# Query, key and value projections by seven products in pairs, instead of twelve tiles of eight

## The reference, cut to what matters

```python
h = concatenate([meta, x])                  # 16 + 512 = 528 tokens, 1024 channels
xn = rmsnorm(h, norm1_g)
q, k, v, xr, gr, g_merge = split(xn @ w_in) # q: 8 heads of 128, k and v: 2 heads each
q = axial_rope(rmsnorm(q, q_norm_g))        # norm over the 128 channels of a head
k = axial_rope(rmsnorm(k, k_norm_g))
attn = softmax(q k^T * 128**-0.5) v         # each key head serves four query heads
```

## Time and profile before

| | us |
|---|---|
| median of 3 runs | 3007.78 |
| the runs | 3005.63, 3008.38, 3007.78 |
| the profiled execution | 3003.16 |
| its span, first to last instruction | 3001.3 |
| mean granted TensorE clock | 0.969 |

### The profile page before, as it was taken

The page is one execution under the profiler, slowest core; times in us unless marked ns, Lnnn a source line. Parts: engine busy times, 40 slices in busy tenths (PEclk is TensorE's granted clock), DMA queues, the critical chain, the costliest instruction groups (busy, mean ns, idle before and its releaser), DMA issues.

```text
span 3001.3 us, 41615 instructions
## 1 busy us (share of the span) xinstructions
PE 2811.6 (94%) x15208; PEld 1771.2 (59%) x15209; DVE 1423.3 (47%) x2352; ACT 853.8 (28%) x1682; POOL 355.9 (12%) x291
## 2 busy tenths in 40 slices
PE   8999999999999978888989897888999999999999
PEld 5665656788888322222323232225877888888887
DVE  5768677776455211112121221124674788555451
ACT  4546364621212211111211121112243544211100
POOL 0101010451001000000000000002113544000000
PEclk9999999999999988999999998898999999999999
DMA  5424425446124899989898989998230221122111
GB/s 228 161 105 131 147 109 200 162 160 247 57 86 171 355 407 399 408 320 402 314 403 360 373 326 410 411 409 328 86 123 17 93 81 71 70 85 85 62 65 60
DMA packets 137444, 636.70 MB, mean 212 GB/s; under 512 B 13232, under 2 KB 56112, under 8 KB 74608
## 3 DMA queue, kind: packets, MB, share of 16 engines
q1 hardware_dynamic: 113136, 579.42, 49.2%
q10 hardware_dynamic: 18688, 36.81, 3.5%
q0 software_dynamic: 5504, 18.88, 1.9%
HBM read 593.82 MB, written 36.44 MB: 210 GB/s over the span
## 4 chain that ended last, share of the span: by engine, by line
PE 80%; DMA 9%; DVE 4%; ACT 3%; issue 2%; POOL 1%; SPq 0%; ACTq 0%; DVEq 0%; POOLq 0%
PE ps L344 30%; PE ps L2874 17%; PE ps L2854 9%; PE ps L2394 9%; DMA slot<-in_w_exp 8%; PE ps L279 2%; PE ps L2541 2%; PE ps L2550 2%; PE ps L3107 1%; PE ps L3090 1%; PE ps L2845 1%; DMA w_modT<-in_w_modT 1%; PE ps L2333 1%; ACT decay L1885 1%; PE ps L2840 1%
## 5 line engine op out<-in xcount | busy, mean ns | idle before, releaser
L2874 PE MATMUL ps<-slot,xT_blk 128*32 128x512 f32 (+1 forms) x3328 | 614.8, 636 | 139.3 <-DMA slot<-in_w_exp 138.8
L2874 PEld LDWEIGHTS ps<-slot,xT_blk 128*32 128x32 f32 (+1 forms) x3328 | 158.9, 127 | 499.2 <-issue 307.0
L2854 PE MATMUL ps<-slot,aT 128*32 128x256 f32 (+1 forms) x2528 | 287.0, 454 | 0.0
L3882 DVE MEMSET b_there<- 128x1 f32 x52 | 3.1, 59 | 495.6 <-DMA b_few<-in_b_gu 483.1
L2854 PEld LDWEIGHTS ps<-slot,aT 128*32 128x32 f32 (+1 forms) x2528 | 111.2, 119 | 184.4 <-issue 153.2
L3886 DVE TENSOR_TENSOR gate<-ps,b_row 128x256 f32<-128x256 f32 (+1 forms) x52 | 29.0, 558 | 343.3 <-PE ps L2874 343.3
L344 PE MATMUL ps<-in_t,in_s 128*128 128x264 f32 x528 | 124.8, 386 | 0.5 <-DVE in_s L435 0.5
L2541 PE MATMUL ps<-hT,slot 128*128 128x512 f32 x256 | 120.5, 603 | 2.2 <-ACT zT L1830 2.1
L2057 ACT ACTIVATE y_row<-ps 128x512 f32<-128x512 f32 (+1 forms) x52 | 25.5, 490 | 333.6 <-PE ps L2854 333.6
L2394 PE MATMUL ps<-h_sum,w_sum 128*128 128x384 f32 (+1 forms) x384 | 120.1, 459 | 0.0
L344 PEld LDWEIGHTS ps<-in_t,in_s 128*128 128x128 f32 x528 | 100.2, 190 | 18.0 <-DVE in_s L435 0.9
(11 more groups left out here) (595 smaller groups left out, 5165.2 us busy)
## 6 DMA issues: line engine op xcount, KB each, us to landing
slot<-in_w_exp SPq DMA_DIRECT2D x384, 1024.0 KB, 11.5
in_w<-in_w_ffn SPq DMA_DIRECT2D x22, 1024.0 KB, 4.8
expert_rows<-zero SPq DMA_DIRECT2D x4, 4608.0 KB, 24.1
slot<-in_w_xbc SPq DMA_DIRECT2D x8, 2048.0 KB, 8.7
sum_here<-sum_rows ACTq DMA_DIRECT2D x32, 512.0 KB, 3.7
w_modT<-in_w_modT SPq DMA_DIRECT2D x16, 1024.0 KB, 4.9
rnn_w<-in_w_rnn SPq DMA_DIRECT2D x16, 1024.0 KB, 4.8
out_w<-in_w_ffn_out SPq DMA_DIRECT2D x8, 1408.0 KB, 8.1
```

Of the source, the lines that this page charges most:

```text
L2854: last = pe.matmul(ps[j * rows:(j + 1) * rows, Y_BANK_OF[s], 0:width], aT[s][:, 2 * half + c, tile * rows:(tile + 1) * rows], slot[4 + k / ...
L2874: last = pe.matmul(GATE_PS[s][tile * rows:(tile + 1) * rows, half, :], xT_blk[:, k, first:first + rows], slot[piece // 4][:, at:at + 512], ...
```

## The change

- Class `Dense` goes; the twelve tiles become six pairs of a `Fast` instance `qkv`: the two key heads (pair 0), four pairs of query heads, the two value heads (pair 5). TensorE's order for pairs 0 and 1 is interleaved by hand.
- `t1` to `t4` are made by VectorE at the start of the stage (`t1` in between the pieces of the last token block), instead of by GpSimd during attention; the recurrent branch uses the same four.
- GpSimd makes `s1` to `s4` of each pair, those of pair 0 ahead of `scaled0`, and its eight-tile sum of squares is cut in two parts between them.
- SP asks for the key/value weights (slot 0) after `turned0`, for the first four query heads' weights (slot 1) after `turned1`, and for the other four (slot 2) after `turned2`.
- The norm's gains go into the tables: ScalarE makes four tables from the loaded one (cosine and sine for keys, cosine and sine for queries). The copies out of PSUM have no gain any more.
- The inverse root of a query head is not multiplied into it. TensorE sums its squares into one column for each of the 34 row tiles of attention (weights: 128 query rows, moving operand: one column of ones), and the inverse root becomes a factor of the maximum and the per-row scale of Exp. Key heads keep the 264-column sums, the reciprocal and the scaling.
- The order of the two value heads' transposes is reversed.

```diff
+    qkv = Fast("qkv", QKV, KD2, H2, qkv_weight, lambda c, l, k: xnT[:, c * KD2 + k, l * H2:(l + 1) * H2],
+               [rnn_t[0][:], rnn_t[1][:], xn_half(0, 1), rnn_t[2][:]],
+               [lambda i: qkv_s[2 * (i % 2)][:], lambda i: qkv_s[2 * (i % 2) + 1][:], lambda i: qkv_weight(i, 1, 0), lambda i: qkv_weight(i, 0, 1)],
+               [0, 1], [2, 3], [6, 7],
...
# SP
         back_pe.after(sp, "turned0")
-        q_in.load(sp)
+        sp.dma_start(slot[0][:], row(io["w_kv"], 0)).then_inc(qkv_loaded[0][0], 16)
         back_pe.after(sp, "turned1")
-        kv_in.load(sp)
+        load_q(0)
+        load_q(1)
+        back_pe.after(sp, "turned2")
+        load_q(2)
+        load_q(3)
...
# ScalarE
+        take("first11", "p1", 0, 0, 0)
+        take("first11", "p1", 1, 0, 0)
+        act.wait_ge(s_rope, 16)
...
+        rot_act.done(act.activation(k_table[:, 0], rope[:, 0], ACT.Copy, scale=gain(1)), "k_cos")
+        rot_act.done(act.activation(k_table[:, 1], rope[:, 1], ACT.Copy, scale=gain(3)), "k_sin")
...
+        for i in range(2, QKV):
+            act.wait_ge(rot_dve.sem, rot_dve.at(f"out{i - 2}_0"))
+            take("first12", "p6", i, 0, 1)
+            turn(i - 1, 0)
+            act.wait_ge(rot_dve.sem, rot_dve.at(f"out{i - 2}_1"))
+            take("first22", "p7", i, 1, 1)
+            if i + 1 < QKV:
+                act.wait_ge(rot_dve.sem, rot_dve.at(f"out{i - 1}_0"))
+                take("first11", "p1", i + 1, 0, 0)
...
# TensorE
+        qkv.p1(pe, 0, qkv_loaded[0])
         sum_squares(3)
...
+        back_act.after(pe, "root2")
+        qkv.p2(pe, 0)
+        qkv.p1(pe, 1, qkv_loaded[1])
+        back_act.after(pe, "root3")
+        qkv.p2(pe, 1)
+        qkv.dve.after(pe, "t1")
+        qkv.p5(pe, 0)
+        qkv.dve.after(pe, "t2")
+        qkv.p6(pe, 0)
+        qkv.p5(pe, 1)
+        qkv.dve.after(pe, "t3")
+        qkv.p7(pe, 0)
...
+        def row_sums(i, tiles):
+            pe.wait_ge(rot_act.sem, rot_act.at(f"square{i - 1}_0"))
+            for g in tiles:
+                r0, n = tile_rows(g)
+                r0 -= g // KV_TILES * KV_ROWS
+                last = pe.matmul(ps[0:n, 5, ROW_COL + g:ROW_COL + g + 1], square_flat[:, r0:r0 + n], ones[:, 0:1], start=True, stop=True)
+            rot_pe.done(last, f"rows{i}")
...
+        for i in range(2, QKV - 1):
+            qkv.p6(pe, i)
+            qkv.p1(pe, i + 1, qkv_loaded[i + 1])
+            qkv.p7(pe, i)
+            qkv.p5(pe, i + 1)
+            if i == 2:
+                k_sum(0)
+            row_sums(i, row_tiles[i])
+            qkv.p4(pe, i)
+            qkv.p2(pe, i + 1)
+            qkv.p3(pe, i)
...
# VectorE
+            if k == KD2 - 1:
+                back_dve.after(dve, f"scaled3_{k}")
+                back_pool.after(dve, "scaled1")
+                qkv.dve.done(dve.tensor_tensor(rnn_t[0][:], xn_half(0, 1), xn_half(0, 0), ALU.subtract), "t1")
...
# GpSimd
+        qkv_sum_12(0)
+        qkv_sum_3(0)
         for t in range(2):
             back_dve.after(pool, f"inverse{t}")
...
+        qkv_sum_12(1)
+        back_act.after(pool, "square3a")
+        add_squares(range(1, KD2))
+        qkv_sum_4(0)
+        qkv_sum_3(1)
+        back_act.after(pool, "square3b")
+        add_squares(range(KD2, KD))
+        qkv_sum_4(1)
+        for i in range(2, QKV):
+            qkv_sum_12(i)
+            qkv_sum_3(i)
+            qkv_sum_4(i)
         back_pe.after(pool, "sum3")
```

More of the change, by code:

```diff
@@ new lines, in _, with k_sum @@
+        qkv.p7(pe, 0)
+        qkv.p6(pe, 1)
+        qkv.dve.after(pe, "t4")
+        qkv.p4(pe, 0)
+        qkv.p3(pe, 0)
+        def k_sum(r):
+            pe.wait_ge(rot_act.sem, rot_act.at(f"square0_{r}"))
+            if r == 0:
+                pe.wait_ge(rot_act.sem, rot_act.at("k_root1"))
+            for p in range(2):
+                last = pe.matmul(ps[:, 4 + p, 0:H2], ones, square_k[:, r, p * H2:(p + 1) * H2], start=True, stop=True)
+            rot_pe.done(last, f"k_sum{r}")
+        def row_sums(i, tiles):
[5 more added lines that the diff above has]
+            rot_pe.done(last, f"rows{i}")
@@ L3978, in _ @@
+        rot_dve.all(dve)
         for g in ATTN_STEPS:
```

486 lines of the change are left out of this document (251 added, 235 removed).

## The result

The changed kernel took 3009.9 us in the median of 12 runs (3008.2 to 3014.8); the kernel before, on the same chip, 3005.8 us in 12 runs (2999.9 to 3008.7). The ratio is 1.0019, with a 95% interval of 1.0010 to 1.0028: 4.1 us more by the medians, 5.8 by the means, near my 3008.0 and within its range. The profiled execution has a span of 3006.4 us, against 3001.3. The total came out; the parts it was made of did not.

What follows compares the result with a forecast made beforehand. TensorE, busy 94% of the span, was taken as the bound, fed by expert-row gathers until 2100 us. Terms -10.1 - 1.8 + 2.0 + 9.2 + 0.9 = +0.2 gave 3008.0 us, range 2999 to 3014.5.

Steps and rivals of the forecast that it cites:

- TensorE's content: First query product to first attention score: fewer matmul records take TensorE's work from 97.0 to 86.9 us, -10.1.
- old waits gone: Same stage: TensorE's 1.16 us wait for ScalarE's copy and most small ones at the start vanish, -1.8 us.
- Waits that come, at the start of the products: First pairs' products: TensorE waits for VectorE's t1 and t2, slowed beside GpSimd, +2.0 us (0 to 4.5).
- If every t waits out one GpSimd operation: Full-wait case at the start of the products: TensorE waits 1.3 us before p5_0 and 3.2 before p6_0.
- Rival 4: GpSimd and VectorE in turns, full 4.5 us at the start, 1.5 in key pairs: +4.0, 3012.0 us, chance 0.10.
- The moved loads: Before the first product: earlier key/value weights delay the last expert-row gather, and so TensorE, by +9.2 us (6.4 to 10.0).
- SP asks at turned0 (2076.42): Moved-loads step: at that time SP requests 2 MB of key/value weights instead of query weights, with gathers still moving.
- Nothing is slack in there: Chain up to 2100 us, gathers to first query product: delaying the last gather delays TensorE by the same time.
- Rival 1: Gathers don't care about the moved loads; last one lands within 2.5 us of before: 2998.8 us, chance 0.20.
- Attention: Maximum's tensor product and per-row Exp scale cost the same kind of instruction; small operations hide: 0 to +0.5 us.
- The clock: TensorE idles about 6 us before the last token block, lowering its granted clock afterwards: +0.9 us (0 to 1.7).
- Rival 3: Broken stretch before 2109 us leaves TensorE at 1.2 GHz well into the pairs: 3021 us, chance 0.13.

Runs made afterwards that it cites:

- e6: e3 with twelve gathers of the last three token tiles fetching 256 columns, not 1024, the rest zero-filled by GpSimd (rows not the reference's): 2998.7 us, one execution.
- e7: e3 with the key/value weights asked for right behind the last expert's down products, not after the first tile's turning: 2999.8 us, ratio to the kernel before 0.9977.
- e2: The changed kernel with part of GpSimd's sums and additions of squares put behind VectorE's t4: 3000.6 us, ratio to the kernel before 0.9981.
- e3: The changed kernel with both edits, row maximum by a scalar operand and GpSimd's sums and additions behind t4: 2999.4 us, ratio to the kernel before 0.9976.
- e5: e3 with constant factors in attention's maximum and exponential, leaving out the normalization of the queries: 2995.7 us, ratio to the kernel before 0.9959.
- e9: The changed kernel, unchanged, run again for a second profile: 3009.8 us, ratio to the kernel before 1.0021.
- e8: The kernel before, unchanged, run again for a second profile: 3006.2 us, one execution.
- e4: The kernel before with its query weights asked for one token block later, after turned1, not turned0: 3008.0 us, ratio to the kernel before 1.000.
- e12: e3 with the key/value weights asked for one block later, after turned1 with the query weights right behind: 2997.4 us, ratio to the kernel before 0.9965.
- e10: e1 run a second time, beside e9: 3010.0 us against 3009.8.
- e1: The changed kernel with attention's row maximum multiplied by a scalar operand again, not as a product of two tensors: 3010.2 us, ratio to the kernel before 1.0018.

## Why the forecast held, and what in it did not

**TensorE's content, -10.1, and old waits gone, -1.8: right.** Where nothing stands in its way, the second stretch is 87.2 us (e6, e7) to 88.4 (e2, e3, e5) against 98.8, so 10.4 to 11.6 less, for 11.9 forecast. All of the 1.2 us between the two is one wait for ScalarE's copy, here in e3:

```profile
2142.22 2.02 PE L258 MATMUL ps<-xnT,slot 128*128 128x264 f32 x8 [1.19 <-ACT qkv_raw L2072]
```

**Waits that come, at the start of the products, +2.0 (0 to 4.5): mechanism right, size wrong, and outside its own bounds.** 97.6 less 88.4 is 9.2 us. It is 7.0 of waits and 3.4 of low clock behind them, less the 1.2 us for ScalarE's copy, which the changed kernel doesn't wait for. The step that failed is "If every t waits out one GpSimd operation (+1.27), and each half of the scaling too". It is not each half that waits, but each of its eight pieces. The Trainium skill (GPSIMD Engine Reference, section Specifications) has VectorE instructions with two SBUF inputs share GpSimd's interface; the trace agrees, down to a 128x1 product (0.94 us beside GpSimd, 0.16 else). I had weighed this with one wait per tensor. Counting instructions, 8 + 2 at about 1.0 us each, would have put t2 10 us later.

**Rival 4 was this mechanism**, priced at +4.0 in sum with 0.10. It deserved more of both: the waits at the start alone came to 7.0 against its 4.5. The key pairs, where it had 1.5, showed no wait over 0.25 us.

**The moved loads, +9.2 (6.4 to 10): true in one of the profiles, hidden in the others.** In e9 the last use, counted from the first gather, is 9.3 us later than in the kernel's first profile and 7.7 later than in the earlier trace rows, and the first product 7.7 later too. The packet arithmetic was sound: the Trainium skill (DMA: Bandwidth & Descriptors, section Queues, rings and completion order) has an engine go round its queues packet by packet, and 24 packets to 18 agree. In the seven other profiles with this load and full gathers it comes 30.7 to 33.4 us behind the first gather. The step that failed is "SP asks at turned0 (2076.42)": I took one time from one profile, in which TensorE had no gaps; there it is 16.2 us behind the first gather, in e8 23.2. The first product came 39.9 us behind the first gather in that profile, 43.5 and 42.5 in e8 and e4, and 41.5 to 47.6 in eleven of the changed kernel and its variants. A second step failed with it, "Nothing is slack in there, so what delays the last gather delays TensorE by the same time". From the last use to the first product it is 7.5 to 7.6 us in the first profile of before, in e9 and in e6, but 9.8 to 14.1 us in the eleven others; in e7 the last use comes 2.2 us later than in e3 and the first product does not. So some 6 us of delay can be lost there. e12 and e4 put the loads later, and against the kernels that they edit their medians move by -2.0 and +1.8 us. By the estimate under e10, the kernel before starts its first product at 2102.8 us (2102.3 on e9's chip), the changed one at 2100.7 (2100.3): in the median the term is not +9.2 but about -2, for a reason that stays open. Rival 1 was right for the profile that was taken, and the forecast for the next.

**Attention, 0 to +0.5: wrong, +5.7.** The step is "a tensor product in place of a scaling on 128x1 and a per-row scale of Exp cost the same kind of instruction". e1 and e5 split it: 3.3 us for the product of two tensors, stretched beside GpSimd, of which 1.7 are the clock behind the waits that it makes, and 2.4 for operands that are columns and not constants (0.09 us on 34 exponentials is 3.1 us of ScalarE, 0.06 on 34 products 2.1 of VectorE, on a chain that TensorE waits for in part). A cost per instruction of a tenth of a microsecond is no zero when the loop is a chain.

**The clock, +0.9**: 3.4 us of the 9.2 (0.74 in the mean from 2110 to 2123), 1.7 in the attention and 1.7 at the end, behind other waits than I thought. Rival 3 fell: from 2123.99 on the products run at 1.78 us.

**What nobody forecast: the end.** From the recurrent branch's first product to the end is 707.8 us in e1, e9, e10, e6 and the first profile of the changed kernel, 706.1 in the nine others. The window of the changed kernel where it shows (columns: busy of PE, PEld, DVE, ACT, POOL, granted clock, DMA share, GB/s), and the same piece of work in the kernel before:

```profile
2875.00:2885.00 10.00, 9.04 (x33) 7.47 (x34) 9.97 (x4) 0.00 (x0) 0.00 (x0) 0.83 0.01 2
```
```profile
2871.60:2881.60 10.00, 9.04 (x41) 7.77 (x42) 9.97 (x4) 0.00 (x0) 0.00 (x0) 1.00 0.01 2
```

The granted clock is 0.83 in the mean of these 10 us, so partly at the 1.2 GHz level, where it is 1.00 before: 10 x 0.17 = 1.7 us, the whole difference. A wait of 1.91 us for VectorE ends at 2875.96; the kernel before has the same wait of 1.91 us there, without the drop. So the wait alone does not bring it, and why it comes in those five and not in the others I did not test.

**The sum, by its own terms.** On the first two profiles: -1.2 (products, waits and clock together), +5.7, +1.7, and +1.8 between the first gather and the first product, less 2.9 by which this execution had reached the first gather earlier, makes the 5.1 us of the span. In the median execution, by the estimate under e10, it is -1.2, +5.7, +1.7 and -2.1, together the 4.1 us measured. Forecast: -9.0, 0, 0 and +9.2. The -1.2 was forecast as -9.0: the waits came to 7.0 for 2.0, the clock to 3.4 for 0.9, and the content was 0.3 over mine. So the total was right by luck: the largest loss on my list, 9.2, stayed away in seven of the eight profiles with this load and full gathers, while the waits and the clock at the start, the attention and the end cost 7.5, 5.7 and 1.7 us more than I had for them. That it lay in the range is no proof of the argument.

## What to carry to other kernels

Ask of every VectorE instruction with two SBUF operands what GpSimd does at that moment, and count instructions, not tensors: eight small pieces pay eight times, and a 128x1 product on a chain lost up to 1.07 us, a 128x1056 subtraction 0.95. Where VectorE is on the critical path, the cheap cure is to make GpSimd wait some microseconds for it (9.9 in e2), not to speed anything up. Such waits of TensorE can cost a second time, in granted clock (3.4 us behind 7.0 us of waits here). Before a forecast rests on the order of two events a few microseconds apart, such as a load and the gathers it collides with, take the time that separates them as a draw: a single profile of the kernel before was 3.6 us off its own second one there, and both cases of the collision turned up in two profiles of the changed kernel.

## What the runs showed of the hardware beyond that

Beside gathers that fill the DMA engines TensorE got its matmuls in small groups, 0.7 or 1.43 us apart, with 1.4 to 3.1 us of gaps in sum, in 11 of 14 profiles, near the time at which a 16 KB instruction packet is moved; not in the first profile of before, in e6 and in e7, where such a packet is moved as well (2076 to 2078 in the first two, 2080 to 2082 in e7), for no reason that I found. With them, signals of matmuls that the profile shows as done came up to 6 us late. That the gathers hold up its instructions is argued from this, not shown. The price of GpSimd beside VectorE is not confined to two inputs. The scaling of the probabilities, with one tensor input of 128x528, takes at most 0.50 us in any profile where no GpSimd operation lies beside it; beside GpSimd it took 1.34 to 1.51 us in the changed kernel, 0.49 to 1.19 in e1, e10 and e3, and 0.50 to 1.31 in the kernel before. VectorE's timeline in the kernel before, and in e10, with GpSimd on the same sums:

```profile
2263.78 0.84 DVE L3994 TENSOR_SCALAR probs<-probs,row_sum 128x528 f32<-128x528 f32 x1
2266.08 1.31 DVE L3994 TENSOR_SCALAR probs<-probs,row_sum 128x528 f32<-128x528 f32 x1
```
```profile
2253.55 0.21 DVE L4047 TENSOR_SCALAR row_max<-row_max,r_neg 128x1 f32<-128x1 f32 x1
...
2253.86 0.49 DVE L4055 TENSOR_SCALAR probs<-probs,row_sum 128x528 f32<-128x528 f32 x1
```
